# Values of a pair of heads in three pieces, and gate stores and reloads earlier on SyncE, in a two-block transformer kernel

## The chip, the cores and the metric

The kernel runs on one core of one Trainium2 chip. The metric is device time of one execution in microseconds (us), as the median of several. TensorE is PE in the profile, its weight loads PEld, VectorE DVE, ScalarE ACT, GpSimd POOL, SyncE SP.

## What is computed

Two transformer blocks on 512 tokens of width 1024, all in float32. The first block has a causal attention of 8 heads with forget gates ("f" in the kernel) and a second one of 8 heads with 2 key groups ("n"), made of three branches: compressed blocks, selected blocks and a window. Cut to the core:

```python
s = einsum('bhqd,bkhd->bhqk', qi, k) * SCALE + ci[..., None] - c[:, :, None, :]
o_fox = einsum('bhqk,bkhd->bqhd', masked_softmax(s, causal), v)
o_nsa = sum over (cmp, slc, win) of gate * softmax(q k^T + bias) v
merged = sigmoid(g_a) * (o_fox @ w_br_fox) + sigmoid(g_b) * (o_nsa @ w_br_nsa)
x = x + merged @ w_out;  x = x + relu(h @ w_ff1)**2 @ w_ff2
```

The second block puts 16 meta tokens in front, has a sliding window attention with sinks (half "A", 8 heads, 2 key heads) and a sparse attention over the 256 best keys of an indexer (half "B", 8 heads on a latent of 128), merged in the same way and followed by a gated MLP:

```python
o_a = sliding_window_sink_attention(aq, ak, av, sinks, bias_a)
o_b = indexed_sparse_mla(q_abs, c_kv, iq, ik, iw, w_uv, bias_b)
mixed = gate_a * (o_a @ w_branch_a) + gate_b * (o_b @ w_branch_b)
h = h + mixed @ w_out
h = h + (silu(hn @ w_ffn_gate) * (hn @ w_ffn_up)) @ w_ffn_down
```

## The kernel before, in words

Weights come as tiles of 128 x 1024 in a fixed order (`tile_list`). `sync_program` (L495 on) loads tile j into one of 4 raw buffers WR (L500); that waits until tile j-4 has been split. ACT casts a tile to its high part WH (`split_to`, L1146), DVE (L1604) or POOL (L2248) subtracts for the low part WL; there are 3 pairs of these, each free when its tile's matmuls are done. Each product is high*high + high*low + low*high (L543 is the helper of all plain matmuls, so most rows have this line).

An attention is a pipeline of units, one unit for one head and one block of 128 query rows (qt = 3, 2, 1, 0, from long to short). Eight units make a group: two heads, four row blocks. All engines walk the same counter t. At step t, PE writes the scores of units t and t+1 (even t; `scores1`, `scores2`) to PSUM and transposes unit t-6 (D_T = 6; `transposes1` L722, `transposes2` L852). DVE adds the bias and takes the row maximum (`maxima1` L1719, `maxima2` L1807), takes the reciprocal of unit t-1 (L1813), and copies the transposed units 0 and 1 of each group out of PSUM (L1822 in the second attention). ACT copies the other transposed units (`copies1` L1229, `copies2` L1278) and takes the exponential of unit t (L1218, L1268). POOL multiplies by the reciprocal (L2301; L2405 and, for meta tokens, L2404) and, in half A, puts the sink behind each row (L2378). In the second attention the weights of the meta tokens have transposes of their own after a group's last unit (L860, L863).

The values of a whole group (`values1`, `values2`) follow at t = 8j+15 (D_V = 8), when all its transposed units are copied: PE multiplies them with V for row blocks m = 0 to 3 and both heads, 512, 384, 256 and 128 columns (in A: 256, 256, 256, 128), into one PSUM bank, bank 5 in the first attention and 6 in the second. `values_c` and the last matmul of `values2` add the compressed branch and the meta tokens. One step later ACT copies the bank to Bh (`high1` L1233, L1300) and DVE subtracts for Bl (`low1`, L1847). Before each pair, `values` waits for Bl of the pair ahead, since it writes the same bank.

In the second attention the first half (t < 32) is A, the second B. At t = 32 DVE turns the indexer's scores into a mask SMK (L1836), which PE adds to B's scores. SMK lies over the buffer from which the store of gate 15 reads, so that DVE waits for that store. In the same step, ahead of it, DVE splits the branch tiles br2 0 to 2.

The gates of the second block's merge (16 tiles, ga2 and gb2) are computed before the second attention, copied by ACT (`gate_out`, L1477) to one of 5 buffers GO, stored to HBM by SP (L509) and reloaded after (L519) into G2. In SP's order the store of gate n stands ahead of the load of tile gate_tile(n)+7, the first four reloads ahead of gate_tile(15)+8. The tiles at the end of this part are g12, g13, uq, g14, ukv, g15, br2 0 to 7, wo2 0 to 7. ACT writes the keys of B (L1544, behind the copies of its values, L1199) over gate buffers, and waits for the stores of gates 0 to 14 first; DVE's low keys (L2175) and POOL's copies of keys (L2366) follow.

Of the kernel before, what the change touches and what calls it, by code (L numbers as in the profile page):

```python
# [86 lines left out]
def build(nc, d, out):  # L87
# [20 lines left out]
    with ExitStack() as ctx:  # L108
# [133 lines left out]
        PT2 = {"A": [(AHL, 0), (AHL, 896), (AHL, 1792), (AHL, 4960)], "B": [(AHL, 0), (AHL, 1664), (AR, 12992), (AR, 14656)]}  # L242
# [129 lines left out]
        D_T, D_V = 6, 8  # L372
        SC1 = (0, 1, 2, 6)
# [38 lines left out]
        U2 = 64  # L412
# [77 lines left out]
        def sync_program(sp):  # L490
# [30 lines left out]
            out_at = {gate_tile(n) + 7: n for n in range(16)}  # L521
            in_at = {tid["br2", i] + 5: i for i in range(2, 8)}
            for j in range(2, len(tiles)):
                if j in out_at:
                    gate_out(out_at[j])
                if j == gate_tile(15) + 8:
                    for n in range(4):
                        gate_in(n)
                if j in in_at:
                    for n in (2 * in_at[j], 2 * in_at[j] + 1):  # L530
                        gate_in(n)
                weights(j)
# [8 lines left out]
        def tensor_program(pe):  # L541
# [183 lines left out]
            def values1(j):  # L725

                x, p, br = groups1[j]
                pair = p + (4 if x == "n" else 0)
                copied1(8 * j + 1)
                copied1(8 * j + 7)  # L730
                if pair and br < 2:
                    pe.wait_ge(p_lo, pair)
                for m in range(4):
                    for w in range(2):
                        h, (X, c0) = 2 * p + w, turned_at(j, w)
                        v = FV[:, m, 64 * h:64 * h + 64] if x == "f" else V2[:, m, 128 * br - 128 + 64 * (h // 4):128 * br - 64 + 64 * (h // 4)]
                        last = mm(bank(5)[hrows(h), 128 * m:T], v, X[:, c0 + 512 * m:c0 + 512 + 384 * m], m == 0 and br < 2,
                                  m == 3 and br == 0)
                last.then_inc(p_pv, 1)
# [49 lines left out]
            def attention1():  # L789
                for t in range(U1 + D_V + 1):  # L790
                    if t < U1 and t % 2 == 0:
                        scores1(t)
                    compressed(t)
                    if 0 <= t - D_T < U1:
                        transposes1(t - D_T)
                    if t >= D_V and (t - D_V) % 8 == 7:
                        j = (t - D_V) // 8
                        values1(j)
                        if groups1[j][0] == "n" and pair_of(j) is not None:
                            values_c(pair_of(j) - 4)  # L800
# [65 lines left out]
            def values2(j):  # L866

                x, p = "AB"[j // 4], j % 4
                copied2(8 * j + 1)
                copied2(8 * j + 7)  # L870
                if j:
                    pe.wait_ge(r_lo, j)

                for m in (0, 2, 1, 3) if x == "A" else range(4):
                    for w in range(2):
                        h, (X, c0) = 2 * p + w, turned2_at(j, w)
                        o = bank(6)[hrows(h), :]
                        if x == "A":
                            n = 256 if m < 3 else 128
                            mm(o[:, 128 * m:128 * m + n], AV[:, m, 64 * (h // 4):64 * (h // 4) + 64],  # L880
                               X[:, c0 + 256 * m:c0 + 256 * m + n], m == 0, False)
                        else:
                            mm(o[:, 128 * m:T], VB[:, m, 64 * h:64 * h + 64], X[:, c0 + 512 * m:c0 + 512 + 384 * m], m == 0, False)
                pe.wait_ge(r_mc, j + 1)
# [6 lines left out]
            def attention2():  # L891
                for t in range(U2 + D_V + 1):
# [4 lines left out]
                    if t >= D_V and (t - D_V) % 8 == 7:  # L897
                        values2((t - D_V) // 8)
# [233 lines left out]
        def scalar_program(ac):  # L1132
# [115 lines left out]
            def attention1():  # L1248
                for t in range(U1 + D_V + 2):
# [5 lines left out]
                    if t > D_V and (t - D_V - 1) % 8 == 7 and pair_of((t - D_V - 1) // 8) is not None:  # L1255
                        high1(pair_of((t - D_V - 1) // 8))
# [13 lines left out]
            def copies2(i):  # L1270
# [4 lines left out]
                if j > 1:  # L1275

                    ac.wait_ge(r_pv, 4 if j == 4 and i % 2 else j - 1)
# [11 lines left out]
            def attention2():  # L1289
                for t in range(U2 + D_V + 2):  # L1290
# [6 lines left out]
                    if t > D_V and (t - D_V - 1) % 8 == 7:  # L1297
                        pair = (t - D_V - 1) // 8
                        ac.wait_ge(r_pv, pair + 1)
                        ac.copy(Bh[:, pair, :], bank(6)).then_inc(r_hi, 1)  # L1300
                    if t == U2 // 2:
# [290 lines left out]
        def vector_program(dv):  # L1592
# [191 lines left out]
            def attention1():  # L1784
                for t in range(U1 + D_V + 2):
# [7 lines left out]
                    if t > D_V and (t - D_V - 1) % 8 == 7 and pair_of((t - D_V - 1) // 8) is not None:  # L1793
                        low1(pair_of((t - D_V - 1) // 8))
# [20 lines left out]
            def copies2(i):  # L1815
# [5 lines left out]
                dv.wait_ge(r_pv, 4 if i == 33 else j - 1)  # L1821
                dv.tensor_copy(turned2(i), bank(4 + i % 2)[:, 0:128 * blocks2(i)].rearrange("p (a c) -> p a c", c=128)).then_inc(r_cd, 1)  # L1822

            def attention2():
                for t in range(U2 + D_V + 2):
                    if t == U2 // 2:
# [17 lines left out]
                    if t > D_V and (t - D_V - 1) % 8 == 7:  # L1844
                        pair = (t - D_V - 1) // 8
# [386 lines left out]
        def pool_program(pl):  # L2232
# [130 lines left out]
            pl.wait_ge(h_hi.sem, h_hi.end("kb"))  # L2363
            for h in range(H):
# [198 lines left out]
```

## Time and profile before

| | us |
|---|---|
| median of 3 runs (1681.53 to 1683.13) | 1681.69 |
| the profiled execution | 1689.02 |
| its span, first to last instruction | 1687.2 |
| PE busy, of the span | 1571.0 (93%) |
| mean granted TensorE clock | 0.952 |

The profile is that of one execution, which took 7.3 us more than the median; all rows come from it. PE is busy for 93% of the span as an average over all stages. The first attention lies at 175 to 334 us, the second at 1072 to 1206 us, with half B from 1120 us on. Times in a timeline count from the span's start. A row's last part in brackets is the time in which the engine had stood idle before it, with what released it.

### The profile page before, as it was taken

How to read it: one execution, taken by the hardware profiler on the slowest of the kernel's cores; microseconds unless marked ns; L12 is line 12 of the kernel's file. 1: busy time of each engine (PE TensorE's matmuls, PEld its weight loads, DVE VectorE, ACT ScalarE, POOL GpSimd, SP SyncE). 2: the span in 40 equal slices, each digit the busy share in tenths (PEclk: the TensorE clock that was granted, in tenths of full speed). 3: DMA queues.
4: the chain of work that ended last, by engine and by line, in shares of the span. 5: the costliest groups of instructions: out<-in, count | busy, mean ns of one | idle time of the engine just before them, and what ended most of it. 6: DMA issues, size and time to landing. Idle time of an engine off the chain costs nothing.

```text
span 1687.2 us, 19470 instructions
## 1 busy us (share of the span) xinstructions
PE 1571.0 (93%) x7178; PEld 1246.8 (74%) x7178; DVE 809.7 (48%) x1556; ACT 624.1 (37%) x1148; POOL 402.1 (24%) x434
## 2 busy tenths in 40 slices
PE   6899988899999999999999999767889999999995
PEld 5787665588877888888887888544567888888884
DVE  5547554444444434333446885443264443443344
ACT  5433454522334222232445434643344322222232
POOL 3200643400010000000036534665432110120112
PEclk9899778999999999999999999768899999999998
DMA  5734200133222332333322943020142233333321
GB/s 188 130 94 117 71 1 14 57 113 94 98 88 79 95 100 89 99 100 99 91 80 88 205 134 113 19 70 7 63 150 89 87 99 100 97 92 99 100 78 60
DMA packets 46526, 153.86 MB, mean 91 GB/s; under 512 B 5682, under 2 KB 5874, under 8 KB 46432
## 3 DMA queue, kind: packets, MB, share of 16 engines
q1 hardware_dynamic: 41696, 137.37, 26.4%
q0 software_dynamic: 4736, 15.25, 4.2%
q8 instruction: 58, 0.95, 0.2%
q14 instruction: 36, 0.29, 0.1%
HBM read 142.51 MB, written 9.55 MB: 90 GB/s over the span
## 4 chain that ended last, share of the span: by engine, by line
PE 82%; DVE 7%; ACT 4%; issue 3%; DMA 2%; POOL 2%; SPq 0%; DVEq 0%; ACTq 0%; POOLq 0%
PE PSA L543 79%; PE PSA L722 2%; ACT AR L1218 1%; DVE WL L1604 1%; PE PSA L852 1%; DMA AHL<-gt_tmp 1%; DVE AR L1694 1%; POOL AR L2405 1%; POOL AHL L2412 1%; DVE AR L1692 1%; DMA gt_tmp<-AR 1%; ACT WH L1146 1%; DMA WR<-w_in 0%; DVE AR L2122 0%; ACT AR L1268 0%
## 5 line engine op out<-in xcount | busy, mean ns | idle before, releaser
L543 PE MATMUL PSA<-Ah,WH 128*128 128x512 f32 x1072 | 427.3, 399 | 22.4 <-DVE WL L1604 18.7
L543 PE MATMUL PSA<-Al,WH 128*128 128x512 f32 x1072 | 421.6, 393 | 0.0
L543 PE MATMUL PSA<-Ah,WL 128*128 128x512 f32 x1072 | 421.3, 393 | 0.0
L1146 ACT CAST WH<-WR 128x1024 fp32r<-128x1024 f32 (+3 forms) x233 | 240.0, 1032 | 224.1 <-PE PSA L543 221.8
L1604 DVE TENSOR_TENSOR WL<-WR,WH 128x1024 fp32r<-128x1024 f32 (+3 forms) x207 | 249.8, 1208 | 82.6 <-ACT WH L1146 82.3
L543 PEld LDWEIGHTS PSA<-Ah,WH 128*128 128x128 f32 x1072 | 204.0, 190 | 69.3 <-issue 22.7
L543 PEld LDWEIGHTS PSA<-Al,WH 128*128 128x128 f32 x1072 | 204.2, 190 | 43.1 <-issue 0.7
L543 PEld LDWEIGHTS PSA<-Ah,WL 128*128 128x128 f32 x1072 | 203.9, 190 | 43.4
L543 PE MATMUL PSA<-Bh,WH 128*128 128x512 f32 x584 | 226.4, 388 | 4.0 <-DVE WL L1604 1.8
L543 PE MATMUL PSA<-Bh,WL 128*128 128x512 f32 x584 | 226.0, 387 | 0.0
L543 PE MATMUL PSA<-Bl,WH 128*128 128x512 f32 x576 | 223.6, 388 | 0.0
L2242 POOL TENSOR_TENSOR AR<-AR 128x512 f32<-128x512 f32 x36 | 51.5, 1439 | 588.3 <-ACT AR L1164 587.9
L543 PEld LDWEIGHTS PSA<-Bh,WH 128*128 128x128 f32 x584 | 109.7, 188 | 28.3 <-issue 3.8
L543 PEld LDWEIGHTS PSA<-Bh,WL 128*128 128x128 f32 x584 | 109.7, 188 | 22.2
L543 PEld LDWEIGHTS PSA<-Bl,WH 128*128 128x128 f32 x576 | 108.2, 188 | 22.3
L2419 POOL TENSOR_TENSOR AR<-AR 128x512 f32<-128x512 f32 x22 | 47.4, 2154 | 282.4 <-DVE AR L2204 282.4
L543 PE MATMUL PSA<-ARR,WH 128*128 128x512 f32 (+4 forms) x288 | 86.9, 388 | 5.8 <-DVE WL L1604 5.8
L2248 POOL TENSOR_TENSOR WL<-WR,WH 128x1024 fp32r<-128x1024 f32 x26 | 62.5, 2410 | 86.0 <-ACT WH L1146 86.0
L2039 DVE TENSOR_TENSOR XT<-PSA,XT 128x512 f32<-128x512 f32 x32 | 22.1, 691 | 107.8 <-PE PSA L543 107.8
L543 PEld LDWEIGHTS PSA<-ARR,WH 128*128 128x128 f32 x288 | 54.0, 195 | 17.4 <-issue 7.1
L722 PE MATMUL PSA<-CST,AR 128*128 128x128 f32 x240 | 48.9, 325 | 16.5 <-ACT AR L1229 11.3
L1218 ACT ACTIVATE AR<-AR 128x512 f32<-128x512 f32 (+3 forms) x96 | 54.2, 567 | 25.5 <-DVE AR L1719 25.4
(359 smaller groups left out, 1993.5 us busy)
## 6 DMA issues: line engine op xcount, KB each, us to landing
WR<-w_in SPq DMA_DIRECT2D x228, 512.0 KB, 3.5
gt_tmp<-AR SPq DMA_DIRECT2D x16, 256.0 KB, 4.5
AHL<-gt_tmp SPq DMA_DIRECT2D x16, 256.0 KB, 4.1
WR<-w_in SPq DMA_DIRECT2D x8, 384.0 KB, 3.0
XT<-scr_tmp POOLq DMA_DIRECT2D x8, 264.0 KB, 15.1
XT<-xT_in SPq DMA_DIRECT2D x4, 512.0 KB, 8.3
XT<-scr_tmp POOLq DMA_DIRECT2D x8, 256.0 KB, 13.9
XT<-xT_in POOLq DMA_DIRECT2D x1, 2048.0 KB, 10.2
```

The lines of the kernel that those rows point to most:

```text
L543: return pe.matmul(o, l, r, start=start, stop=stop)
L722: last = pe.transpose(bank(3 + i % 2)[:, 128 * m:128 * m + 128], E1[i % 8][:, 128 * m:128 * m + 128], ident)
L852: last = pe.transpose(bank(4 + i % 2)[:, 128 * m:128 * m + 128], E2[x][i % 8][:, c0:c0 + 128], ident)
L1146: ac.copy(WH[p][:, 0:n], WR[j % RAW][:, 0:n]).then_inc(w_hi, 1)
L1218: ac.activation(E, E, ACT.Exp, bias=NMX1[:, c:c + 1], scale=-1.0, accum_out=RSM1[:, c:c + 1]).then_inc(p_ex, 1)
L1604: dv.tensor_tensor(WL[p][:, 0:n], WR[j % RAW][:, 0:n], WH[p][:, 0:n].bitcast(F), ALU.subtract).then_inc(w_lo, 1)
L1692: dv.max(mx8[qt], S).then_inc(k_top, 1)
L1694: dv.match_replace(S, mx8[qt], S, NREP).then_inc(k_top, 1)
L2039: dv.tensor_tensor(x3[:, i, 0:T], bank(i % 2), x3[:, i, 0:T], ALU.add).then_inc(f_ad, 1)
L2242: pl.tensor_tensor(acc, acc, sq[(k - 1) % 3], ALU.add).then_inc(n_ac.sem, 1)
L2248: pl.tensor_tensor(WL[p][:, 0:n], WR[j % RAW][:, 0:n], WH[p][:, 0:n].bitcast(F), ALU.subtract).then_inc(w_lop, 1)
L2419: pl.tensor_tensor(ZR[s], RT[2 * s], RB["m2"], ALU.mult).then_inc(u_zr, 1)
```

## The change

The values of a pair are issued in three pieces (row blocks 0; 1; 2 and 3; in A 0; 2; 1 and 3) at t = 8j+15, 8j+17 and 8j+19, among the transposes and scores of later groups, in both attentions. Bh and Bl follow at t = 8j+20 instead of 8j+16. The buffers of B's transposed units are ordered anew, and the copies of B's first group wait for the values of A's third pair instead of its last. DVE's (and ACT's) split of br2 0 to 2 stands at t = 12 instead of t = 32. On SP the store of gate n stands ahead of tile gate_tile(n)+5 (n < 12) or +4, the first four reloads ahead of gate_tile(15)+5. POOL waits for its own last split before it copies keys.

```diff
-        PT2 = {"A": [(AHL, 0), (AHL, 896), (AHL, 1792), (AHL, 4960)], "B": [(AHL, 0), (AHL, 1664), (AR, 12992), (AR, 14656)]}
+        PT2 = {"A": [(AHL, 0), (AHL, 896), (AHL, 1792), (AHL, 4960)], "B": [(AHL, 0), (AR, 12992), (AHL, 1664), (AR, 14656)]}
...
+
+        PIECES = {0: 0, 2: 1, 4: 2}
+        D_E = D_V + 5
...
-            out_at = {gate_tile(n) + 7: n for n in range(16)}
+
+            out_at = {gate_tile(n) + (5 if n < 12 else 4): n for n in range(16)}
             in_at = {tid["br2", i] + 5: i for i in range(2, 8)}
             for j in range(2, len(tiles)):
                 if j in out_at:
                     gate_out(out_at[j])
-                if j == gate_tile(15) + 8:
+                if j == gate_tile(15) + 5:
                     for n in range(4):
                         gate_in(n)
...
-            def values1(j):
+            def values1(j, piece):
 
                 x, p, br = groups1[j]
                 pair = p + (4 if x == "n" else 0)
-                copied1(8 * j + 1)
-                copied1(8 * j + 7)
-                if pair and br < 2:
-                    pe.wait_ge(p_lo, pair)
-                for m in range(4):
+                if piece == 0:
+                    copied1(8 * j + 1)
+                    copied1(8 * j + 7)
+                    if pair and br < 2:
+                        pe.wait_ge(p_lo, pair)
+                for m in ((0,), (1,), (2, 3))[piece]:
                     for w in range(2):
                         h, (X, c0) = 2 * p + w, turned_at(j, w)
                         v = FV[:, m, 64 * h:64 * h + 64] if x == "f" else V2[:, m, 128 * br - 128 + 64 * (h // 4):128 * br - 64 + 64 * (h // 4)]
                         last = mm(bank(5)[hrows(h), 128 * m:T], v, X[:, c0 + 512 * m:c0 + 512 + 384 * m], m == 0 and br < 2,
                                   m == 3 and br == 0)
-                last.then_inc(p_pv, 1)
+                if piece == 2:
+                    last.then_inc(p_pv, 1)
...
                     if t < U1 and t % 2 == 0:
                         scores1(t)
                     compressed(t)
                     if 0 <= t - D_T < U1:
                         transposes1(t - D_T)
-                    if t >= D_V and (t - D_V) % 8 == 7:
-                        j = (t - D_V) // 8
-                        values1(j)
-                        if groups1[j][0] == "n" and pair_of(j) is not None:
+
+                    j, o = divmod(t - D_V - 7, 8)
+                    if 0 <= j < len(groups1) and o in PIECES:
+                        values1(j, PIECES[o])
+                        if PIECES[o] == 2 and groups1[j][0] == "n" and pair_of(j) is not None:
                             values_c(pair_of(j) - 4)
...
+            def values2(j, piece):
...
+                if piece == 0:
+                    copied2(8 * j + 1)
+                    copied2(8 * j + 7)
+                    if j:
+                        pe.wait_ge(r_lo, j)
+
+                for m in (((0,), (2,), (1, 3)) if x == "A" else ((0,), (1,), (2, 3)))[piece]:
...
+                if piece < 2:
+                    return
                 pe.wait_ge(r_mc, j + 1)
...
-                    if t >= D_V and (t - D_V) % 8 == 7:
-                        values2((t - D_V) // 8)
+                    j, o = divmod(t - D_V - 7, 8)
+                    if 0 <= j < U2 // 8 and o in PIECES:
+                        values2(j, PIECES[o])
...
-                    if t > D_V and (t - D_V - 1) % 8 == 7 and pair_of((t - D_V - 1) // 8) is not None:
-                        high1(pair_of((t - D_V - 1) // 8))
+                    if t > D_E and (t - D_E) % 8 == 7 and pair_of((t - D_E) // 8) is not None:
+                        high1(pair_of((t - D_E) // 8))
...
-                    ac.wait_ge(r_pv, 4 if j == 4 and i % 2 else j - 1)
+                    ac.wait_ge(r_pv, j - 1)
...
-                    if t > D_V and (t - D_V - 1) % 8 == 7:
-                        pair = (t - D_V - 1) // 8
+                    if t > D_E and (t - D_E) % 8 == 7:
+                        pair = (t - D_E) // 8
                         ac.wait_ge(r_pv, pair + 1)
                         ac.copy(Bh[:, pair, :], bank(6)).then_inc(r_hi, 1)
-                    if t == U2 // 2:
+                    if t == 12:
                         split_to(tid["br2", 2])
...
-                    if t > D_V and (t - D_V - 1) % 8 == 7 and pair_of((t - D_V - 1) // 8) is not None:
-                        low1(pair_of((t - D_V - 1) // 8))
+                    if t > D_E and (t - D_E) % 8 == 7 and pair_of((t - D_E) // 8) is not None:
+                        low1(pair_of((t - D_E) // 8))
...
-                dv.wait_ge(r_pv, 4 if i == 33 else j - 1)
+                dv.wait_ge(r_pv, j - 1)
...
-                    if t == U2 // 2:
+                for t in range(U2 + D_E + 1):
+                    if t == 12:
                         split_to(tid["br2", 2])
                     top_run(2)
...
-                    if t > D_V and (t - D_V - 1) % 8 == 7:
-                        pair = (t - D_V - 1) // 8
+                    if t > D_E and (t - D_E) % 8 == 7:
+                        pair = (t - D_E) // 8
                         dv.wait_ge(r_hi, pair + 1)
                         dv.tensor_tensor(Bl[:, pair, :], bank(6), Bh[:, pair, :].bitcast(F),
                                          ALU.subtract).then_inc(r_lo, 1)
...
+            pl.wait_ge(w_lop, lo_no[gate_tile(15)])
```

## Rows read from the trace of the kernel before

**Rows 1.** Windows: length, busy by engine, then PEclk (granted clock), DMA, GB/s.

```profile
175.00:334.00 159.00, 137.18 (x746) 92.73 (x748) 84.82 (x354) 83.53 (x281) 80.13 (x111) 0.83 0.05 16
1072.00:1112.50 40.50, 33.31 (x183) 23.96 (x183) 21.07 (x99) 27.13 (x97) 32.35 (x71) 0.75 0.00 1
...
1120.20:1203.00 82.80, 63.42 (x301) 37.52 (x303) 27.43 (x110) 32.79 (x104) 47.49 (x71) 0.76 0.04 13
```

**Rows 2.** Waits of PE, first attention: total us, times, longest.

```profile
PE PSA L722 <- ACT AR L1229: 11.3, 17, 1.0
PE PSA L722 <- ACT WW L1229: 4.3, 7, 1.4
```

**Rows 3.** Waits of PE, second attention.

```profile
PE PSA L543 <- DVE AR L1807: 11.6, 7, 2.4
PE PSA L543 <- DVE AR L1836: 7.6, 1, 7.6
...
PE PSA L852 <- ACT AHL L1278: 5.6, 9, 1.3
```

**Rows 4.** Timeline of PE, first attention: start, us, instruction, idle before.

```profile
192.06 2.38 PE L543 MATMUL PSA<-AR 128*64 128x512 f32 x16
...
298.65 0.41 PE L722 MATMUL PSA<-CST,AR 128*128 128x128 f32 x2 [0.98 <-ACT AR L1229]
...
304.00 3.36 PE L543 MATMUL PSA<-AR 128*64 128x512 f32 x16
```

**Rows 5.** Chain of waits, first attention: start, us.

```profile
296.83 0.82 ACT AR L1218 x2
297.65 0.48 ACT Bh L1233
```

**Rows 6.** Timeline of all engines, half B.

```profile
1163.85 0.57 ACT L1300 CAST Bh<-PSA 128x512 fp32r<-128x512 f32 x1
...
1164.46 0.69 DVE L1847 TENSOR_TENSOR Bl<-PSA,Bh 128x512 fp32r<-128x512 f32 x1 [1.49 <-ACT Bh L1300]
...
1165.83 1.08 PE L543 MATMUL PSA<-ARR 128*128 128x400 f32 x3 [2.42 <-DVE AR L1807]
...
1169.97 0.60 PE L863 MATMUL PSA<-CST,AHL 128*64 128x128 f32 x4
...
1171.03 1.56 POOL L2405 TENSOR_SCALAR AR<-AR 128x512 f32<-128x512 f32 x1
```

**Rows 7.** Timeline of PE, ahead of the second attention.

```profile
1064.03 0.79 PE L543 MATMUL PSA<-Ah,WH 128*128 128x512 f32 x1 [3.36 <-DVE ARR L2175]
```

**Rows 8.** Timeline of ACT, ahead of the second attention.

```profile
1036.28 0.59 ACT L1477 COPY AR<-PSA 128x512 f32<-128x512 f32 x1 [2.42 <-PE PSA L543]
...
1042.20 1.05 ACT L1146 CAST WH<-WR 128x1024 fp32r<-128x1024 f32 x1
...
1052.60 0.59 ACT L1477 COPY AR<-PSA 128x512 f32<-128x512 f32 x1 [4.23 <-PE PSA L543]
...
1061.33 4.90 ACT L1544 ACTIVATE ARR<-PSA 64x512 fp32r<-64x512 f32 x8 [4.29 <-DMA gt_tmp<-AR]
```

**Rows 9.** Chain of waits, ahead of the second attention.

```profile
1057.05 4.09 DMA gt_tmp<-AR
```

**Rows 10.** Timeline of DVE at t = 32.

```profile
1110.33 3.48 DVE L1604 TENSOR_TENSOR WL<-WR,WH 128x1024 fp32r<-128x1024 f32 x3
1118.94 1.07 DVE L1836 TENSOR_SCALAR AR<-AR 128x144 bf16<-128x144 f32 x4 [5.14 <-DMA gt_tmp<-AR]
```

**Rows 11.** Timeline of POOL at t = 32.

```profile
1109.58 0.92 POOL L2405 TENSOR_SCALAR AHL<-AHL,AR 128x256 f32<-128x256 f32 x1
1110.45 1.13 POOL L2378 COPY AHL<-AR 128x1 f32<-128x1 f32 x1
1111.55 2.96 POOL L2405 TENSOR_SCALAR AHL<-AHL,AR 128x256 f32<-128x256 f32 x1
```

**Rows 12.** DMA issues of the page: KB each, median us to landing.

```profile
WR<-w_in SPq DMA_DIRECT2D x228, 512.0 KB, 3.5
```

More of the change, by code:

```diff
@@ L789, in attention1 @@
             def attention1():
-                for t in range(U1 + D_V + 1):
+                for t in range(U1 + D_E):
                     if t < U1 and t % 2 == 0:
@@ L864, in transposes2 @@
                     last.then_inc(r_mt, 1)
-            def values2(j):
+            def values2(j, piece):
                 x, p = "AB"[j // 4], j % 4
[L869 to L874, printed above, removed]
+                if piece == 0:
[4 more added lines that the diff above has]
+                for m in (((0,), (2,), (1, 3)) if x == "A" else ((0,), (1,), (2, 3)))[piece]:
                     for w in range(2):
@@ L891, in attention2 @@
             def attention2():
-                for t in range(U2 + D_V + 1):
+                for t in range(U2 + D_E):
                     if t < U2 and t % 2 == 0:
@@ L1248, in attention1 @@
             def attention1():
-                for t in range(U1 + D_V + 2):
+                for t in range(U1 + D_E + 1):
                     if 0 <= t - D_T < U1:
@@ L1289, in attention2 @@
             def attention2():
-                for t in range(U2 + D_V + 2):
+                for t in range(U2 + D_E + 1):
                     if 0 <= t - D_T < U2:
@@ L1784, in attention1 @@
             def attention1():
-                for t in range(U1 + D_V + 2):
+                for t in range(U1 + D_E + 1):
                     if t < U1:
@@ L1819, in copies2 @@
                 dv.wait_ge(r_tr, i + 1)
-                dv.wait_ge(r_pv, 4 if i == 33 else j - 1)
+                dv.wait_ge(r_pv, j - 1)
                 dv.tensor_copy(turned2(i), bank(4 + i % 2)[:, 0:128 * blocks2(i)].rearrange("p (a c) -> p a c", c=128)).then_inc(r_cd, 1)
             def attention2():
-                for t in range(U2 + D_V + 2):
-                    if t == U2 // 2:
+                for t in range(U2 + D_E + 1):
+                    if t == 12:
                         split_to(tid["br2", 2])
```

## Prediction

> **What bounds the kernel now.** I read the windows of both attentions first, then TensorE's (PE's) waits there, its timeline, the chain, and the timelines of the other engines. Outside these stages the change touches only gate stores. The windows [rows 1] show that neither attention is full: PE is idle for 159.0-137.2 = 21.8 us of the first, 7.2 us of its half A in the second, 19.4 us of half B. The granted clock is 0.83, 0.75 and 0.76; it has two levels, 2.4 and 1.2 GHz, so 54, 20 and 40 us (twice the missing share times the window), 114 us in all, pass at 1.2 GHz.
>
> In the first attention PE waits above all for ScalarE's (ACT's) copies out of PSUM: 11.3+4.3 us [rows 2]. In the second it waits 11.6 us for maxima of VectorE (DVE), 7.6 us once for the mask (L1836) and 5.6 us for ACT [rows 3]; in B it also waits for GpSimd (POOL). The timeline shows where: the values of a pair are one burst, 2.38 us at 2.4 GHz, 3.36 us where the clock was low at its start, then comes the next group's work, and the waits stand in its tail, 0.98 us ahead of one transpose [rows 4]. During the burst ACT and DVE run dry; after it they are the chain: an exponential 0.82 us, then the pair's copy to Bh 0.48 us [rows 5], then the copy for which PE waits.
>
> **Part 1, first attention.** Added and removed matmuls: none. Of 1280 columns per head, 512 stay in the old place, 384 move two units later and 384 four units later: 60% of 2.38 us, 1.43 us per group at 2.4 GHz. Scores and exponentials after the burst start that much earlier, and the pieces stand where PE waited. High and low halves (copy to Bh, subtraction to Bl) move four units later, out of the wait of 0.98 us into the tail. That returns a part: ACT then has 0.48 us more ahead of the last copy of the group. Of the 15.6 us of waits for ACT I take two thirds, **-10**. Bounds: -3 (only Bh's 0.48 us in six or seven groups) to -20.9 (all of PE's idle time but its start). The middle is nearer the rows, since ACT's exponentials and copies stay and become almost continuous.
>
> **Part 2, half A.** The same move meets waits for ACT of 5.6 us, nine in the tails of three groups [rows 3], so 1.87 us a tail; two of these tails follow a burst. POOL too loses time there, as its first normalisation of a group waits for DVE, which waits for Bh. Two tails at 1.75 us: **-3.5**, bounds 0 and -7.2 (PE's idle time in A).
>
> **Part 3, half B.** Four times PE stops 2.25 to 2.43 us in the scores of the second row block, as in the row at 1165.83, since maximum 33 of the next group stands behind Bl on DVE, which waits for Bh on ACT [rows 6]: 9.5 us of the 11.6. The change puts Bh and Bl four units later. What is late next: the same pair of copies (0.57+0.69 us) and an exponential then stand ahead of the last scores of the group, up to 2 us. There PE already waits for POOL, whose normalisation of the next group's unit can start only after the meta transposes (L863 at 1169.97, POOL at 1171.03, 1.56 us each [rows 6]), so that most of it is hidden. **-8.5**, bounds -4 (half comes back) and -9.7. The copies of B's first group no longer wait for A's last values; costed at nothing, hidden by the PE work behind them.
>
> **Part 4, the join ahead of the second attention.** PE waits 3.36 us for DVE's low keys (L2175), and its first matmul behind that took 0.79 us, so at the low clock [rows 7]. Behind it is ACT, which ends its value copies at 1057.04 and starts the keys (L1544) at 1061.33, 4.29 us later, released by a gate store; gate 14 had been copied out (L1477) at 1052.60+0.59 = 1053.19 [rows 8]. the chain has SP's store only at 1057.05, 4.09 us long [rows 9]; it stood behind weights. At +4 it issues near 1053.3 and lands, with the same 4.1 us, at 1057.4. Keys, POOL's shifted keys behind them and gate 15 move up by 3.4 to 3.9 us; gate 15 also starts without an idle stretch ahead of it, and so, I estimate, at the high clock, which gives about 1 us more. **-4.8**, bounds -3.4 and -5.0.
>
> **Part 5, the mask at t = 32.** DVE splits three branch tiles for 3.48 us at 1110.33 and then waits 5.14 us for the store of gate 15, which on SP stands behind the weights that this split frees [rows 10]. With the store at +4 and the split at t = 12 both are gone. Left is the mask itself, 1.07 us, ahead of the next scores: **-6.5** of the 7.6, bounds -5 and -7.6.
>
> **Part 6, the split at t = 12.** The 3.48 us of DVE are now inside A, where POOL's normalisations are close to the bound. Beside this split a normalisation on POOL took 2.96 us where its neighbour took 0.92, and a copy of one column 1.13 us [rows 11]: 2.0 plus about 1.0, so 3.0 us lost on POOL, at the same time as DVE's own stop. **+3.0**, bounds 0 (PE has work in hand) and +3.5. The Trainium skill (SBUF — State Buffer, Who interferes with whom) has it that a VectorE instruction with two SBUF inputs and a GpSimd instruction that reads SBUF exclude each other for a whole instruction; by that rule three subtractions could hold POOL for all 3.5 us. The row agrees in kind; the sum goes by its 3.0.
>
> **Part 7, the ends and SP.** At the end of each attention the pieces have fewer units to stand between; PE's last waits go, V of the last pair waits for Bl a little: **-0.5**, bounds +1 and -1.2. Loads behind an earlier store now wait for its gate. The tightest is the tile ukv behind gate 12, copied out by 1036.87 [rows 8]: with 3.5 us to landing [rows 12] it is there at 1040.5 for a cast at 1042.20 [rows 8], 1.7 us to spare, and PE needs it 10 us later. Cost nothing; if the cover is gone, each late load would cost its lateness. Reloads of gates come earlier, into an idle queue; their user, POOL after the attention, is not waiting. POOL's added wait is on its own finished work: nothing.
>
> **Sum**: -10 -3.5 -8.5 -4.8 -6.5 +3.0 -0.5 = -30.8 us. The profiled execution took 1689.0 us, 7.3 us over the median of 1681.7; the sum holds against either, and on the median gives 1650.9.
>
> **Rivals.**
> *ACT and DVE bind again.* Bh moved into the tail delays the last copies of each group; Part 1 gives 3, Part 3 gives 4, A 2, the ends nothing: 3+2+4+4.8+6.5-3.0 = 17.3, **1664.4**. For it: ACT's copies are the releaser now. Against: ACT is busy only 83.5 of 159 us [rows 1].
> *The clock rises.* With less idle time a third of the 114 us at 1.2 GHz goes: 38 us, at half the work each, with five sixths of it not hidden, about 15: **1636**. For it: the low burst at 304.00 stands behind a tail with waits [rows 4]. Against: the clock is no higher where PE is busier, 0.75 at 82% in A and 0.76 at 77% in B [rows 1].
> *Slower: the burst was what brought the clock back.* The burst of 3.36 us began low and ended high: all high it is 2.38, all low it would be near twice that [rows 4]. Cut in three between transposes and short scores, there may be no such stretch. Now 282-114 = 168 us run at 2.4 GHz, PE 83% busy. The gain of 30.8 is used up when 37 us of these fall to 1.2 GHz; if half do, 84 us, it costs 70 less the 15 that idle time still hides: **1706**. Against: the burst at 192.06 took 2.38 us [rows 4], so the clock had come back before it. The Trainium skill (TensorE: Matmul & The Clock Gate, Part 4) says that transposes do not count as busy for the clock in the way that matmuls do, and speaks for this rival.
> *Nothing net*: if the split in A held POOL and PE for each subtraction and the tails stayed, 1681. The waits of Parts 4 and 5 hang on a store whose place on SP is seen, so this is unlikely.
>
> **Numbers.** Forecast 0.50; ACT and DVE again 0.25; clock up 0.17; clock down 0.05; nothing 0.03. All bounds at their weak ends (3, 0, 4, 3.4, 5, less 3.5 and 1) give 1670.8, at their strong ends (20.9, 7.2, 9.7, 5.0, 7.6, 0, 1.2) 1630.1. Range 1635 to 1669: it leaves out half of the clock-up case's fast side, the slower case and the weakest corner. Faster by over 0.2% (about what a measurement of this kernel can tell from no change, 3.4 us): 0.93; within: 0.02; slower: 0.05.
>
> **What would show it.** No wait for L1836 above 1.5 us; none for L2175; ACT's L1544 right behind L1199; no stop of 2.4 us in the scores of B's second row block, but a wait for maxima ahead of the last block; DVE's L1604 near unit 12 with slow POOL rows beside it; waits for ACT in the first attention at 5 to 8 us. A clock below 0.83 and 0.75 in the windows, or waits for ACT as before, would make it wrong.

## The result, and the profile after

The changed kernel takes 1639.3 us (median of 4 runs, 1635.8 to 1642.7), the kernel before in the same session 1682.4 us: ratio 0.9735, 95% interval 0.9702 to 0.9768, 43 us less. It is inside the range, 11.6 us below the forecast of 1650.9, and 3 us above the rival in which the clock rises. The profiled execution took 1638.6 us, with a span of 1636.8 us. The profiled execution of before lay 7 us above its median, at a mean clock of 0.952 (its six longest executions in the experiments lie at 0.951 to 0.955, its six shortest at 0.957 to 0.959), so the stage differences below add up to 50 us, not 43.

The windows of the changed kernel, from the first maxima of each stage to its last Bl (half A: to the mask); the columns are those of [rows 1]:

```profile
175.40:310.10 134.70, 123.82 (x746) 79.75 (x746) 83.85 (x354) 85.86 (x283) 79.52 (x108) 0.94 0.07 22
1039.30:1075.70 36.40, 27.77 (x166) 19.68 (x164) 22.27 (x100) 25.46 (x95) 33.26 (x71) 0.81 0.28 95
1075.70:1158.00 82.30, 70.16 (x334) 39.92 (x335) 28.41 (x116) 34.90 (x109) 53.27 (x76) 0.77 0.07 26
```

The same three stages of the kernel before:

```profile
175.80:336.10 160.30, 138.48 (x747) 93.19 (x746) 84.67 (x354) 84.18 (x283) 79.57 (x109) 0.83 0.06 20
1072.70:1118.90 46.20, 32.67 (x180) 23.26 (x178) 22.35 (x100) 26.43 (x97) 34.65 (x70) 0.74 0.13 39
1118.90:1207.00 88.10, 67.46 (x320) 39.67 (x321) 28.53 (x115) 33.97 (x106) 51.17 (x73) 0.77 0.10 34
```

Each row can be split in two. A window less PE's busy time is idle time: waits. The matmuls are the same in both kernels (747 and 746 records in the first attention, 500 and 500 in the second), so I read a change of PE's busy time as the clock. In the second attention that holds for both halves together only: 180 matmuls lay ahead of the mask before and 166 after, so 14 changed halves. In the first attention the idle time falls from 160.3-138.5 = 21.8 us to 134.7-123.8 = 10.9 us, and the busy time from 138.5 to 123.8 us. Waits gave 10.9 us there and the clock 14.7 us. Time at 1.2 GHz (twice the missing share of the clock) fell from 54 to 16 us. In both halves of the second attention together idle time fell from 34.2 to 20.8 us (13.4 us) and busy time from 100.1 to 97.9 (2.2 us). From the last Bl of the first attention to the first maxima of the second it is 7.4 us less (736.6 to 729.2), of which the join, from the first gate copy to the maxima, is 145.2-139.4 = 5.8 (3.7 us less idle time and 2.1 us less busy time). Before, between and behind these lie the other 3.4 us.

PE's waits after, the whole span (engine, instruction <- releaser: us in total, times, longest); they answer to [rows 2, 3]:

```profile
PE PSA L547 <- DVE AR L1819: 9.6, 6, 2.2
PE PSA L859 <- ACT AHL L1290: 6.0, 7, 3.3
...
PE PSA L726 <- ACT AR L1241: 3.2, 6, 0.7
PE PSA L547 <- DVE AR L1848: 2.5, 1, 2.5
...
PE PSA L726 <- ACT WW L1241: 2.0, 3, 1.1
```

The waits for ACT's copies in the first attention are a third of [rows 2]: 5.2 us for 15.6. The mask, now L1848, holds PE 2.5 us for 7.6. The maxima, now L1819, hold it 9.6 us for 11.6: this term hardly moved. POOL, which held PE 7.8 us in the second attention before, holds it 1.3 us. The wait for low keys of [rows 7] is gone. ACT's timeline at the join, for [rows 8], shows why:

```profile
1024.32 0.59 ACT L1489 COPY AR<-PSA 128x512 f32<-128x512 f32 x1 [4.23 <-PE PSA L547]
1024.80 2.00 ACT L1158 CAST WH<-WR 128x1024 fp32r<-128x1024 f32 x2
1026.70 2.06 ACT L1211 ACTIVATE AR<-PSA 128x512 f32<-128x512 f32 x4
1028.65 1.83 ACT L1556 ACTIVATE ARR<-PSA 64x512 fp32r<-64x512 f32 x3
```

The keys (L1556) start right behind the value copies (L1211). Half B, for [rows 6]: PE, DVE and ACT ahead of the last row block's scores of a group.

```profile
1105.35 0.60 PE L870 MATMUL PSA<-CST,AHL 128*64 128x128 f32 x4
1105.72 0.33 PE L547 MATMUL PSA<-ARR 128*128 128x144 f32 x1
1107.92 0.90 PE L547 MATMUL PSA<-ARR 128*128 128x144 f32 x3 [1.87 <-DVE AR L1819]
```

```profile
1106.82 0.69 DVE L1859 TENSOR_TENSOR Bl<-PSA,Bh 128x512 fp32r<-128x512 f32 x1 [1.08 <-ACT Bh L1312]
1107.43 0.43 DVE L1819 CUSTOM_DVE_ANT_0 AHL<-PSA,XT 128x272 f32<-128x272 f32 x1
```

```profile
1105.70 0.52 ACT L1280 ACTIVATE AHL<-AHL,AR 128x272 f32<-128x272 f32 x1
1106.13 0.19 ACT L1280 ACTIVATION_READ_ACCUMULATOR AHL<-AHL,AR 128x1 f32 x1
1106.22 0.56 ACT L1312 CAST Bh<-PSA 128x512 fp32r<-128x512 f32 x1
```

The stop is the old one, four units later: PE waits for a maximum, which stands behind Bl, which waits for Bh, which stands behind an exponential. At unit 12 of half A, for [rows 10, 11], DVE's split and POOL beside it:

```profile
1050.45 3.73 DVE L1616 TENSOR_TENSOR WL<-WR,WH 128x1024 fp32r<-128x1024 f32 x3
```

```profile
1050.37 0.91 POOL L2418 TENSOR_SCALAR AR<-AR 128x256 f32<-128x256 f32 x1
1051.24 0.72 POOL L2391 COPY AHL<-AR 128x1 f32<-128x1 f32 x1
1051.93 2.96 POOL L2418 TENSOR_SCALAR AR<-AR 128x256 f32<-128x256 f32 x1
```

The same instruction takes 0.91 us and, beside the split, 2.96 us. But PE does not wait for it: its waits for POOL in half A are 0.6 us before and after. What PE waits for is DVE itself, through ACT:

```profile
1054.11 0.47 DVE L1819 CUSTOM_DVE_ANT_0 AHL<-PSA,AR 128x256 f32<-128x256 f32 x1
```

```profile
1054.62 0.51 ACT L1280 ACTIVATE AHL<-AHL,AR 128x257 f32<-128x257 f32 x1 [3.37 <-DVE AR L1819]
1055.04 0.19 ACT L1280 ACTIVATION_READ_ACCUMULATOR AHL<-AHL,AR 128x1 f32 x1
1055.13 0.24 ACT L1290 COPY AHL<-PSA 128x128 f32<-128x128 f32 x1
```

```profile
1055.52 0.66 PE L859 MATMUL PSA<-CST,AR 128*128 128x128 f32 x2 [3.28 <-ACT AHL L1290]
```

The maximum stands behind the split on DVE, the exponential waits 3.37 us for it, the copy stands behind the exponential, and PE waits 3.28 us for the copy: the longest of the 6.0 us for L1290.

### The profile page after: what moved, and what is told of

The parts are those of the page before. It is cut to its first block, busy times and chain, and to the rows that moved or that the text cites. A ratio compares the mean times of both kernels' runs of the same rounds, so it can differ in the third digit from the quotient of the medians.

```text
span 1636.8 us, 19471 instructions
## 1 busy us (share of the span) xinstructions
PE 1550.2 (95%) x7178; PEld 1227.6 (75%) x7178; DVE 807.7 (49%) x1556; ACT 625.7 (38%) x1148; POOL 402.5 (25%) x434
## 4 chain that ended last, share of the span: by engine, by line
PE 84%; DVE 6%; ACT 3%; issue 2%; DMA 2%; POOL 2%; SPq 0%; DVEq 0%; ACTq 0%
PE PSA L547 82%; PE PSA L726 2%; PE PSA L859 1%; DVE WL L1616 1%; DMA AHL<-gt_tmp 1%; ACT AR L1230 1%; ACT WH L1158 1%; DMA WR<-w_in 1%; DVE AR L1706 0%; POOL AR L2418 0%; POOL AHL L2425 0%; DVE AR L1704 0%; DVE AR L1731 0%; DVE AR L2240 0%; POOL ARR L2379 0%
## 5 line engine op out<-in xcount | busy, mean ns | idle before, releaser
L547 PE MATMUL PSA<-AR 128*64 128x512 f32 (+10 forms) x220 | 64.3, 478 | 1.5 <-DVE AR L2121 1.0
## 6 DMA issues: line engine op xcount, KB each, us to landing
XT<-xT_in POOLq DMA_DIRECT2D x1, 2048.0 KB, 10.2
```

Source lines behind the costliest of these rows:

```text
L547: return pe.matmul(o, l, r, start=start, stop=stop)
```

## The experiments

In every kernel below piece 3 means all four blocks of a pair's values in one burst, as before, and D_E1 and D_E2 are the change's D_E for the first and the second attention. Each was timed in five rounds against the kernel before on the same chip, in three sessions on three chips. The medians of before were 1681.9 us (pieces or late Bh in the first attention, pieces in the second, gates and split alone), 1684.5 (filler in the tails, split back at 32, later Bl, spread splits) and 1682.9 (the control, undivided second attention, both, both with the first).

**The parts alone.** Pieces in the first attention:

```diff
 # the kernel before, with
+        PIECES1, PIECES2 = {0: 0, 2: 1, 4: 2}, {0: 3}
+        D_E1, D_E2 = 13, 9
```

> The kernel before with the three pieces, and Bh and Bl four units later, in the first attention alone; second attention, store order and split as before. Theory C (the pieces take away some 10 us of waits, and because PE then has no idle tails its clock stays at 2.4 GHz, which gives some 15 us more): the first attention takes about 135 us instead of 160 in the profile, its half-clock stretches sum to 15 to 25 us instead of 54, the whole 20 to 27 us faster. Rival W (the pieces give only the waits, and the clock gain of the changed kernel came from other parts or from chance): 8 to 12 us faster, granted clock in 175 to 309 us still about 0.83.

Measured: 1665.0 us, ratio 0.9897 (0.9876 to 0.9917), 17 us. In its profile the first attention takes 135.6 us at a clock of 0.94, as in the changed kernel. So this part of the change brings the clock by itself, and rival W falls; theory C has the stage and its 16 us at 1.2 GHz right, but the whole, 17 us, lies between the two ranges. In the profile the stage gained 24.7 us. Of the difference 7 us is the profiled before; I can't place it in one stage.

Values undivided, but Bh and Bl late, first attention only:

```diff
+        PIECES1, PIECES2 = {0: 3}, {0: 3}
+        D_E1, D_E2 = 13, 9
```

> The kernel before with the first attention's values still in one burst, but Bh and Bl four units later, as in the change. It tells what the pieces do from what the later Bh does. Theory C (it is the pieces that keep ACT, DVE and PE going): 2 to 6 us faster, half-clock time in the first attention 40 to 54 us. Rival L (the later Bh and Bl, out of the tail's wait, is what lifts clock and time): 15 us faster or more, half-clock time under 30 us.

Measured: 1673.4 us, ratio 0.9945 (0.9925 to 0.9965), 8.5 us. Its first attention, in the windows' columns:

```profile
174.90:321.10 146.20, 125.29 (x746) 84.41 (x746) 84.09 (x353) 84.41 (x283) 79.84 (x108) 0.91 0.06 19
```

Idle time is 20.9 us, for 21.8 before: nearly no wait is gone. Busy time is 125.3 us, for 138.5: 13 us of clock. Time at 1.2 GHz is 26 us. Theory C had the halves wrong: the late Bh gives the clock, and the pieces on top of it (146.2 to 135.6) give 9.5 us of idle time and 1 us of clock. Rival L has the time at 1.2 GHz right (under 30 us), but not the 15 us of the whole. PE's timeline of one tail shows what the late Bh does; first before, then this kernel.

```profile
298.65 0.41 PE L722 MATMUL PSA<-CST,AR 128*128 128x128 f32 x2 [0.98 <-ACT AR L1229]
...
299.51 0.39 PE L543 MATMUL PSA<-CTR,WH 128*128 128x256 f32 x1 [0.22 <-DVE AR L1719]
...
300.70 0.30 PE L722 MATMUL PSA<-CST,AR 128*128 128x128 f32 x1 [0.69 <-ACT AR L1229]
301.57 0.30 PE L722 MATMUL PSA<-CST,AR 128*128 128x128 f32 x1 [0.56 <-ACT AR L1229]
```

```profile
286.82 0.41 PE L726 MATMUL PSA<-CST,AR 128*128 128x128 f32 x2 [0.49 <-ACT AR L1241]
...
288.66 0.30 PE L726 MATMUL PSA<-CST,AR 128*128 128x128 f32 x1 [0.56 <-ACT AR L1241]
...
290.56 0.63 PE L726 MATMUL PSA<-CST,AR 128*128 128x128 f32 x4 [0.51 <-ACT AR L1241]
```

Before, four stops of 2.45 us in all lie within 4 us, and the burst behind them runs low (3.36 us [rows 4]). With the late Bh three stops of 1.56 us lie over as long a stretch, and the burst at 291.12 takes 2.37 us. The stop of 0.98 us is 0.49 without Bh's 0.48 us ahead of the copy; the 0.51 us at 290.56 are new, since Bh now stands ahead of the tail's last copy. This suggested a new theory (K): it is not how much PE idles in a stage, but the crowding of short stops at a group's tail, that brings the clock down. It can't be the whole rule. Before, the next tail has the same four stops (0.98, 0.22, 0.70 and 0.57 us), and the burst behind it is at the full clock:

```profile
326.38 2.38 PE L543 MATMUL PSA<-AR 128*64 128x512 f32 x16
```

The next two kernels test the theory with nothing moved.

Filler in the tails of the kernel before:

```diff
             def transposes1(i):
                 qt = units1[i][3]
+                if i % 8 in (5, 6, 7) and i >= 45:
+                    pe.wait_ge(q_cp, 4)
+                    for u in range(2):
+                        mm(bank(7), QN[u][:, 0:128], KWH[0][:, 0:512], True, True)
                 pe.wait_ge(p_nm, i + 1)
```

> The kernel before with 42 added matmuls of 512 columns (two ahead of the transposes of each of the last three waited-for units of a group, in groups 6 to 12 of the first attention, into a bank that is idle there; nobody reads them). At 2.4 GHz they take 42 x 0.22 = 9.2 us of PE, in places where PE waits for ACT some 0.5 to 1.0 us each time. Theory K (what lowers the clock is the cluster of short waits at a group's tail): the half-clock stretches from 255 us to the end of the first attention shrink from 17 us to under 7, the clock gain pays for the added work, and the first attention is 2 to 5 us shorter in spite of it. Rival N (the clock does not follow the tails' waits; other things move the grid): the half-clock time stays at about 17 us and the first attention is as long as before or up to 5 us longer.

The control, the same matmuls where PE hardly waits:

```diff
+                if i % 8 in (1, 2, 3) and i >= 45:
```

> The control to the filler kernel: the kernel before with 36 of the same added matmuls (36 x 0.22 = 7.9 us at 2.4 GHz), now two ahead of the transposes of units 1, 2 and 3 of groups 7 to 12, where PE hardly waits. Theory K (only work in the clustered waits of the tail keeps the clock up): the tails' waits stay, the half-clock time after 250 us stays at 10 to 17 us, and the first attention is 3 to 9 us longer than before. Rival A (any added PE work between the bursts keeps the clock up, wherever it stands): the half-clock time falls to under 5 us and the first attention is 0 to 6 us shorter, as with the filler in the tails.

Measured: filler in the tails 1677.7 us, ratio 0.9952 (0.9933 to 0.9971), 7 us faster than before with 42 matmuls more; the control 1688.9 us, ratio 1.0028 (1.0014 to 1.0042), 6 us slower. The windows from 255 us to the end of the first attention, of the filler, of the control and of the kernel before:

```profile
255.00:326.60 71.60, 64.98 (x376) 41.19 (x376) 37.47 (x159) 41.15 (x141) 32.30 (x52) 1.00 0.11 36
```

```profile
255.00:336.20 81.20, 70.98 (x367) 47.77 (x368) 37.07 (x158) 40.10 (x139) 32.28 (x52) 0.87 0.13 39
```

```profile
255.00:336.10 81.10, 66.68 (x357) 41.93 (x354) 38.35 (x162) 42.72 (x144) 32.53 (x53) 0.89 0.09 30
```

The windows hold not quite the same matmuls, so it is their clock that compares. With work in the tail's stops it is never low there, and the first attention takes 152.4 us for 160.3. With about the same work elsewhere it is at 0.87 and takes 163.7. The mean clock of whole executions says the same: 0.961 over eight of the filler kernel, 0.956 over twelve of the control and 0.956 for before. Idle time doesn't explain it: the control has 10.2 us of it in its window, less than the 14.4 us of before, and no higher clock. Rivals N and A fall, and theory K holds in kind. In size it was off: the filler's stage gained 7.9 us for the 2 to 5 expected, and the control's time at 1.2 GHz was 21 us for 10 to 17. Shown is that filling the tails' stops lifts the clock and that the same work elsewhere does not; whether the number of the stops, their length or their closeness counts is open. PE's added work of 9.2 us was free: it lay in waits, and paid for itself.

Pieces in the second attention, and beside it the undivided values with late Bh:

```diff
 # second attention's pieces
+        PIECES1, PIECES2 = {0: 3}, {0: 0, 2: 1, 4: 2}
+        D_E1, D_E2 = 9, 13
 # undivided and late
+        PIECES1, PIECES2 = {0: 3}, {0: 3}
+        D_E1, D_E2 = 9, 13
```

> The kernel before with the three pieces in the second attention alone (with its changed places for turned probabilities). The mask still waits for the store of gate 15. Theory M (in half B the wait only moves: the 2.4 us stop in the scores of the second row block becomes a stop ahead of the last block's): half B about 6 us shorter, half A 2 to 3.5 us shorter, the whole 7 to 10 us faster. Rival (the prediction's own step: most of the moved wait is hidden): half B 8 to 9 us shorter, the whole 11 to 13 us faster.

> The kernel before with the second attention's values in one burst, but Bh and Bl four units later (and the turned probabilities' new places). It splits the 8.6 us that the pieces kernel of the second attention gained. Theory M (in half B the late Bh only moves the stop, and it is the pieces that take away the waits for POOL and ACT): 1 to 4 us faster than the kernel before. Rival (the later Bh alone gives it): 7 us faster or more.

Measured: pieces 1673.3 us, ratio 0.9941 (0.9922 to 0.9961); undivided and late 1674.1 us, ratio 0.9937 (0.9915 to 0.9959). They are equal. For the pieces, theory M has the whole (8.6 us) and the moved stop. My theory for the second kernel fell, its rival held: in the second attention, with the gates stored as before, the late Bh alone gives as much, and cutting the values adds nothing that can be measured. Whether it does in the changed kernel wasn't run. Half B (mask to last Bl) of the pieces and of the undivided kernel:

```profile
1113.20:1193.40 80.20, 67.68 (x334) 38.51 (x335) 28.06 (x115) 34.23 (x106) 51.21 (x73) 0.79 0.11 39
```

```profile
1111.50:1190.20 78.70, 63.15 (x316) 36.82 (x321) 28.28 (x115) 33.63 (x106) 51.36 (x73) 0.82 0.11 39
```

The pieces have less idle time (12.5 us for 15.6), the undivided values the higher clock. Over both halves the pieces have 6.9 us less idle and 4.1 us less busy time than before, the undivided values 3.4 and 9.0 (4 of the 500 matmul records are missing there, and this execution, 1670.5 us, lay 3.7 us under its median). In both, PE's waits for POOL in half B fell from 7.2 us to 1.4 and 1.7, and those for maxima only from 10.8 to 8.8 and 9.8.

**Gates and split alone**: the change's lines in SP's order and the split at unit 12, values as before.

```diff
+        PIECES1, PIECES2 = {0: 3}, {0: 3}
+        D_E1, D_E2 = 9, 9
+            out_at = {gate_tile(n) + (5 if n < 12 else 4): n for n in range(16)}
+                if j == gate_tile(15) + 5:
+                    if t == 12:
```

> The kernel before with the earlier gate stores and reloads and the split at unit 12 alone; values undivided in both attentions. Theory S (gate order and mask are on PE's path and additive): first gate copy to first keys 5 us shorter, half A to the mask 4 to 6.5 us shorter (7.6 of the wait gone, less up to 3 lost to the split beside POOL), the whole 8 to 11 us faster. Rival (the parts hide behind waits that only the pieces remove): under 6 us.

Measured: 1670.0 us, ratio 0.9925 (0.9905 to 0.9945), 12 us. Join 5.8 us shorter, half A 6.3 us, nearly as theory S had it (5, 4 to 6.5, and 8 to 11 for the whole); 12 of half A's 180 matmuls now lie behind the mask, and both halves together are 8.9 us shorter. PE's waits from the first maxima of half A to the end of half B:

```profile
PE PSA L547 <- DVE AR L1819: 11.8, 8, 2.4
PE PSA L859 <- ACT AHL L1290: 8.7, 12, 3.3
PE PSA L859 <- POOL AR L2418: 6.6, 7, 1.2
```

No wait for the mask is left, and waits for ACT are 8.7+1.2 us, for 5.6+1.2 before: 3.1 us more, the split's price. Added up, the three parts give 1.03+0.59+0.75 = 2.37% for the change's 2.65, no difference beyond the intervals.

The changed kernel with the split back at unit 32:

```diff
-                    if t == 12:
+                    if t == 32:
```

> The changed kernel with the three branch tiles split at unit 32 again, just ahead of the mask, as before. Theory S (the earlier store of gate 15 alone takes away the 5.1 us wait; the split's 3.5 us of DVE cost about the same in either place, since at unit 12 they meet POOL and ACT at their bound and at unit 32 PE waits for the mask behind them): half A to the mask 0.5 to 1.5 us longer than in the changed kernel, the whole within 2 us of it. Rival (the place at unit 12 is what counts): 3 us slower or more than the changed kernel.

Measured: 1637.9 us, ratio 0.9722 (0.9693 to 0.9750), the same as the changed kernel. The wait for the mask is 5.9 us for 2.5, that for ACT in half A 3.5 for 6.0. DVE doesn't wait for the store there either. What took the 5.1 us away was the earlier store of gate 15; moving the split gave nothing.

**Towards a better version.** Bh and Bl of the second attention one unit later; the three splits one by one in half B; both; both with the first attention's Bh one unit later too:

```diff
+        D_E1, D_E2 = 13, 14                       # later Bl
+                    if t in (42, 50, 58):          # spread splits
+                        split_to(tid["br2", (42, 50, 58).index(t)])
+        D_E1, D_E2 = 14, 14                       # the fourth kernel
```

> The changed kernel with Bh and Bl of the second attention one unit later still, so that DVE takes the last row block's first maxima ahead of Bl. Theory M (the 1.9 to 3.2 us stops in half B are maxima behind Bh and Bl): these stops, 9.9 us in all, fall to under 5, half B is 2 to 5 us shorter than the changed kernel's 82.3 us, and V's first piece waits at most 0.5 us for Bl. Rival (the chain of exponentials and maxima is the bound itself, whatever stands between): the stops come back elsewhere, half B within 1 us of 82.3.

> The changed kernel with the three branch tiles not split together at unit 12 in half A, but one by one at units 42, 50 and 58 in half B. Theory P (in A the split cost about 3 us, because it held POOL and DVE together while both are at their bound): half A 2 to 3.5 us shorter, half B at most 1 us longer, the whole 1.5 to 3 us faster than the changed kernel. Rival Q (the split was hidden in A, or half B loses the same, since weights of the merge arrive later): within 1 us of the changed kernel or slower.

> The changed kernel with both improvements: Bh and Bl of the second attention one unit later, and the three branch tiles split one by one at units 42, 50 and 58. If the two add up (half A 3.5 us from the split, half B 4 to 5 us from the maxima ahead of Bl, less up to 2 because the splits then stand where DVE is wanted), half A to the mask takes about 33 us, half B 76 to 79 us, and the whole is 6 to 10 us under the changed kernel, near 1630. Rival (half B is bound by the pair DVE and POOL, so that the splits eat what the later Bl gives): no faster than the kernel with the splits alone, ratio to before 0.967 or more.

> The same with Bh and Bl of the first attention one unit later too. Theory (the six waits for ACT's copies left in the first attention, 5.2 us in all, are partly Bh ahead of a copy of the tail): the first attention 1 to 3 us shorter than the changed kernel's 134.7. Rival (the copy to Bh then stands ahead of the last copy of the group, as it did before the change in kind, and the clock pays for it): the first attention 2 us longer or more, half-clock time there above 20 us.

| kernel | median us | ratio to before, interval |
|---|---|---|
| changed | 1639.3 | 0.9735 (0.9702 to 0.9768) |
| later Bl | 1636.8 | 0.9716 (0.9690 to 0.9741) |
| spread splits | 1630.3 | 0.9673 (0.9644 to 0.9701) |
| both | 1631.0 | 0.9690 (0.9664 to 0.9717) |
| both, first too | 1634.3 | 0.9696 (0.9672 to 0.9721) |

With the later Bl the stops for maxima are gone, and another is there; PE's waits in half B (1077.0 to 1153.4 us):

```profile
PE PSA L859 <- POOL AR L2418: 6.8, 6, 1.2
PE PSA L547 <- DVE Bl L1859: 2.0, 1, 2.0
PE PSA L547 <- DVE AR L1819: 1.6, 2, 1.0
```

POOL's normalisation is next: 6.8 us, for 0.7 in the changed kernel's half B. Maxima and POOL take turns. From the mask's last instruction on, idle time in half B is 76.4-64.4 = 12.0 us, for 81.3-70.2 = 11.1 in the changed kernel: no wait was gained. Half B was 4.9 us shorter by the clock alone, 0.85 for 0.77, and not all of that need be the edit's: with half B's code unchanged and the split back at 32, half B took 78.2 us at 0.80. The whole is not beyond the intervals, so theory M is right about the place and not about its worth.

The spread splits make half A to the mask's end 33.8 us for 37.4, PE's waits for ACT there 2.9 for 6.0, and no row of POOL is stretched in half B: it stands idle 5.28 us ahead of the group's first unit, where the split at unit 42 falls. That is theory P's gain in half A. Its reason was half right: the stop that went is the one behind DVE's own split, and POOL's stretched row held nobody. For the whole the case is weaker: 9 us by the medians is more than the 3.6 us that a stage shows, the intervals just part (0.9701, 0.9702) and come from different sessions, and that of the kernel with the split back at 32, timed in the same session, overlaps (0.9693). The profiled execution took 1638.0 us, 8 more than the median, at a clock of 0.968 for 0.973 in the mean of the five; the rest isn't placed. Both together aren't better than the splits alone, as the rival had it (0.967 or more); half A took 34.4 us, half B 78.3. In the fourth kernel the waits for ACT's copies fell from 5.2 to 2.1 us, but PE waits 5.4 us for Bl in their place; the first attention took 135.6 us. Its one unit gives nothing, against 133.3 us in the kernel that it was made from.

## Why the prediction was right or wrong

The waits came out nearly as summed, and the clock was missing. Parts 1, 2, 3, 5, 6 and 7 make -26.0 us of waits in the two attentions; idle time fell by 10.9+13.4 = 24.3. Part 4 said -4.8, and the join gave 5.8. Together -30.8 foretold, 30.1 measured, 2.1 of them clock in the join. The rest of the profile's 50 us is 16.9 us of clock in the attentions and 3.4 us outside them. The sum met its waits partly by luck, as Parts 3 and 6 show.

**Part 1** (-10): 10.4 us of the 15.6 us for ACT went, idle time by 10.9. The term of the waits was right. Missing was -14.7 for the clock. The step that failed is the "against" of the rival *The clock rises*: that the clock was no higher where PE was busier, 0.75 at 82% in A and 0.76 at 77% in B. A busy share over a stage is the wrong quantity. The "for" of the same rival, the low burst behind a tail of waits, was the true sign, and the filler and its control show it. The rival had 38 us of low clock go and 15 us for them, over both attentions; in the first attention alone 54-16 = 38 us went, for 14.7 us. That both numbers are met there is chance: over both attentions it was some 51 us for 16.9. It deserved more than 0.17, and not as a rival but as a term beside the waits.

**Part 2** (-3.5): waits for ACT in the second attention went from 6.8 to 3.2 us in the pieces kernel, and to 3.5 in the changed kernel with the split back at 32. Right in size and place. Half A's length doesn't show it: in the pieces kernel it is 46.2-43.1 = 3.1 us shorter because 14 matmuls lie behind the mask, its idle time rose from 13.5 to 14.7 us, and the mask took back 3.5 us (11.1 for 7.6). With undivided values and late Bh, waits for ACT went only to 6.2 us, so here the pieces do take them away.

**Part 3** (-8.5): wrong in its step, and near in size by luck. I had the 9.5 us of stops in the second row block gone, and what comes back "mostly hidden" behind POOL. Waits for maxima went only from 11.6 to 9.6 us; the stop stands ahead of the last block, 1.87 us twice and 0.98+2.22 once. What went is what I took for the cover: POOL's waits, 7.8 to 1.3 us. New are 1.3 us for Bl. Together 7.2 us, for 8.5.

**Part 4** (-4.8): 5.8, its bound was 5.0. Idle time gave 3.7 us, the clock 2.1, where I had about 1. No wait for L2187, L1556 right behind L1211.

**Parts 5 and 6** (-6.5 and +3.0): alone they took 7.6 us of wait for the mask away and brought 3.1 us for ACT. The split's price was right in size, and by luck: I had it from POOL's stretched row and copy, for which PE doesn't wait; it is DVE's own stop, 3.73 us, handed on by ACT as 3.28. And moving the split bought nothing: with it back at unit 32 the mask's wait is 3.4 us longer, ACT's 2.5 shorter, and the whole the same. In the changed kernel 2.5 us of the mask's wait stay, over my limit of 1.5: the mask (1.35 us) begins at 1075.74, behind maxima that stand behind Bl. The Trainium skill (SBUF — State Buffer, Who interferes with whom) has DVE and POOL exclude each other for a whole instruction where, as here, DVE has two inputs in SBUF and POOL reads there; the row, 2.96 us for 0.91, agrees in kind again.

**Part 7** (-0.5) can't be seen apart. *ACT and DVE bind again* (1664.4) didn't happen: ACT's waits in the first attention fell to the 5 to 8 us of the forecast. *The burst brought the clock back* (1706) is refuted: the clock is 0.94 with the burst cut, and 0.91 with it whole and Bh late. By the Trainium skill (TensorE: Matmul & The Clock Gate, Part 4) transposes do not count as busy for the clock as matmuls do. Here cutting the burst and setting the pieces among transposes lowered nothing; whether they count no run here shows.

## What to carry to other kernels

Split a stage's window into PE's idle and busy time before summing: a plan that takes waits away can also change what the same matmuls cost, and each us at 1.2 GHz was worth about 0.4 us in the first attention (14.7 us for 38), and by the profile 0.2 in the second (2.2 us for 13). Look for short stops that lie close together ahead of a heavy burst. Moving a copy of 0.48 us out of such a tail gave the first attention as much as cutting the burst in three on top of it (8.5 and 8.4 us by the medians). When two engines take turns at releasing PE, as DVE and POOL in half B, moving one's work shows the other's wait and gains little. When a row is stretched, look who waits for it before pricing it.

## What was not expected of the hardware

42 matmuls of 512 columns, added where PE waited, made the kernel 7 us faster, since the granted clock in their stretch rose from 0.89 to 1.00; 36 of them elsewhere made it 6 us slower at 0.87. And with nearly the same idle time (20.9 us for 21.8) but Bh moved within the tails, the same stage ran at 0.91 for 0.83. Yet the same four stops stood once ahead of a burst of 3.36 us and once ahead of one of 2.38. Three subtractions of 1.2 us in a row on DVE stretched a normalisation on POOL by 2 us, for which nobody waited; one at a time beside an idle POOL they stretched no row.
